# Three-layer FP32 block on one core: weights loaded per 512 KB unit into six slots, x and the first units alternating, the MLP activation kept in PSUM

## What is computed

```python
# layer 0: s = concat(short gated conv, gated DeltaNet) @ w_out_even; x = layer_norm(alpha * x + s)
#          x = x + (p @ w_pl) * sigmoid(x @ w_pl_gate)
# layer 1: the same with an HGRN2 mixer (w_in_odd: 1024 x 8192, w_out_odd: 2048 x 1024)
# layer 2:
h = h + swa_mixer(rms_norm_2(h, attn_norm), ...)     # sliding window attention, 16 heads
a = jax.nn.relu(rms_norm_2(h, mlp_norm) @ w_up)      # 1024 -> 4096
h = h + (a * a) @ w_down                             # 4096 -> 1024
return rms_norm_2(h, final_norm)
```

## Time and profile before

| what | value |
|---|---|
| time, three runs | 1053.04, 1055.29, 1056.65 us, median 1055.29 |
| the profiled execution | 1055.54 us, its span 1053.8 us (1.7 us lie around the span) |
| busy: PE, PEld, DVE, ACT, POOL | 94%, 88%, 42%, 47%, 67% of the span |
| mean granted TensorE clock | 0.987 of full speed |
| DMA | 146.22 MB in 128940 packets, mean 139 GB/s |

### The profile page before, as it was taken

How to read it: one execution, slowest core, us unless ns; L and a number is a source line. 1 busy time by engine, 2 the same in 40 slices (tenths; PEclk the granted TensorE clock), 3 DMA queues, 4 the chain that set the end, 5 groups by cost and what they waited for, 6 DMA issues and landing times.

```text
span 1053.8 us, 18046 instructions
## 1 busy us (share of the span) xinstructions
PE 993.6 (94%) x7200; PEld 929.7 (88%) x7200; DVE 446.5 (42%) x741; ACT 499.6 (47%) x697; POOL 701.1 (67%) x540
## 2 busy tenths in 40 slices
PE   3699999999999999999999999999997989998996
PEld 3699999989999789999999999888886889887884
DVE  1254854358442153444444444435465264442003
ACT  2465432473224465444555545456547444544430
POOL 2776644556445688856666566659672469999992
PEclk9899999999999999999999999999999999999998
DMA  6989954966823555644444434455541145554651
GB/s 180 189 163 127 125 112 82 118 120 105 140 81 120 177 178 161 191 143 122 128 125 131 137 121 132 139 180 173 168 159 41 50 150 162 160 161 160 212 187 40
DMA packets 128940, 146.22 MB, mean 139 GB/s; under 512 B 8974, under 2 KB 93656, under 8 KB 128856
## 3 DMA queue, kind: packets, MB, share of 16 engines
q1 hardware_dynamic: 125432, 140.05, 52.4%
q10 hardware_dynamic: 3424, 5.01, 1.4%
HBM read 144.00 MB, written 1.05 MB: 138 GB/s over the span
## 4 chain that ended last, share of the span: by engine, by line
PE 73%; POOL 10%; issue 6%; DVE 5%; ACT 3%; DMA 3%; SPq 0%; DVEq 0%; ACTq 0%; POOLq 0%
PE dense L484 18%; PE dense L485 18%; PE dense L486 18%; POOL wlo L461 5%; POOL wlo L460 5%; PE bank L839 4%; DMA raw<-in_w_in_even_dram 3%; PE bank L741 2%; PE bank L736 2%; PE bank L740 2%; PE bank L837 1%; PE dense L553 1%; PE bank L885 1%; DVE nsink L1984 1%; ACT whi L1035 1%
## 5 line engine op out<-in xcount | busy, mean ns | idle before, releaser
L460 POOL TENSOR_TENSOR wlo<-raw,whi 128x512 fp32r<-128x512 f32 x264 | 352.2, 1334 | 312.9 <-ACT whi L1035 310.7
L1035 ACT ACTIVATE whi<-raw 128x1024 fp32r<-128x1024 f32 x264 | 275.1, 1057 | 377.6 <-PE dense L486 247.7
L484 PE MATMUL dense<-x_hi,whi 128*128 128x256 f32 x1232 | 364.9, 296 | 26.1 <-POOL wlo L461 18.8
L461 POOL TENSOR_TENSOR wlo<-raw,whi 128x512 fp32r<-128x512 f32 x264 | 357.4, 1354 | 0.0
L485 PE MATMUL dense<-x_lo,whi 128*128 128x256 f32 x1232 | 352.2, 286 | 0.0
L486 PE MATMUL dense<-x_hi,wlo 128*128 128x256 f32 x1232 | 352.2, 286 | 0.0
L484 PEld LDWEIGHTS dense<-x_hi,whi 128*128 128x128 f32 x1232 | 239.9, 195 | 31.5 <-issue 17.4
L485 PEld LDWEIGHTS dense<-x_lo,whi 128*128 128x128 f32 x1232 | 240.1, 195 | 1.8 <-issue 1.7
L486 PEld LDWEIGHTS dense<-x_hi,wlo 128*128 128x128 f32 x1232 | 239.7, 195 | 0.0
L484 PE MATMUL dense<-whi,ya_hi 128*128 128x512 f32 x192 | 77.9, 406 | 2.9 <-POOL wlo L461 2.2
L486 PE MATMUL dense<-whi,ya_lo 128*128 128x512 f32 x192 | 75.0, 391 | 0.0
(11 more groups left out here) (296 smaller groups left out, 1488.9 us busy)
## 6 DMA issues: line engine op xcount, KB each, us to landing
raw<-in_w_in_odd_dram SPq DMA_DIRECT2D x32, 1024.0 KB, 5.8
raw<-in_w_in_even_dram SPq DMA_DIRECT2D x16, 1024.0 KB, 12.3
raw<-in_w_in_even_dram SPq DMA_DIRECT2D x64, 256.0 KB, 6.1
raw<-in_mlp_w_up_dram SPq DMA_DIRECT2D x16, 1024.0 KB, 5.5
raw<-in_mlp_w_down_dram SPq DMA_DIRECT2D x16, 1024.0 KB, 5.0
raw<-in_w_out_even_dram SPq DMA_DIRECT2D x8, 1024.0 KB, 5.0
raw<-in_w_pl_gate_dram SPq DMA_DIRECT2D x8, 1024.0 KB, 5.2
raw<-in_w_out_odd_dram SPq DMA_DIRECT2D x8, 1024.0 KB, 5.1
```

The source lines that it names most:

```text
L460: pool.tensor_tensor(wlo[:, slot, 0:half], unit_slot(u)[:, 0:half], whi[:, slot, 0:half].bitcast(F32), ALU.subtract)
L461: pool.tensor_tensor(wlo[:, slot, half:2 * half], unit_slot(u)[:, half:2 * half], whi[:, slot, half:2 * half].bitcast(F32), ALU.subtract). ...
L484: pe.matmul(out_, lh, rh, start=start, stop=False, skip_group_check=True)
L1035: act.activation(whi[:, u % NSPL, :], unit_slot(u), ACT.Copy).then_inc(hi_done, 1)
```

## The change

Five things.

1. `raw` has six slots of one unit (the same memory), and every load is of one unit: 264 loads of 512 KB in place of 132 of 1 MB (the conv weights stay at 256 KB per DMA, the k and v weights of attention go from 12 DMAs to 24 of half the size). Before the load of unit u SP waits for `lo_done` of unit u-6.
2. At the start SP issues the first half of x, unit 0, the second half of x, units 1 to 5, then the norm rows. PE transposes both halves of x before unit 0, and ACT takes the high parts of the second half after unit 0 (before: after unit 2).
3. The other 928 KB of the constants are issued by ACT in two parts, 512 KB at step 8 and 416 KB at step 40; DVE waits for the first at step 17 and for the second before the HGRN stage. `tail_turn` moves from step 4 to 6, `gates` from 5 to 7.
4. MLP up: DVE computes `max(x, 0) * root` in place in PSUM (2 x 128x512), ACT squares it in place in PSUM and writes the high part, DVE the low part, all by halves, and the pair is freed after the low part. `rl` is gone.
5. For MLP units POOL computes the low part with one instruction of 128x1024.

```diff
...
 COLS = 512
 RAWK = 4
 SPLK = 2
-NRAW = 3
+NRAW = 6
...
-        raw = sb("raw", [P, NRAW, RAWK * COLS])
+        raw = sb("raw", [P, NRAW, SPLK * COLS])
...
-            return raw[:, (u // 2) % NRAW, (u % 2) * SPLK * COLS:(u % 2 + 1) * SPLK * COLS]
-
-        def weights(c):
+            return raw[:, u % NRAW, :]
...
+            def wide(w):
+                return w[part * RAWK * P:(part + 1) * RAWK * P, :].rearrange("(k p) c -> p k c", p=P)
...
         def _(sp):
-            for c in range(2):
+            def load_x(c):
+
+                cols = slice(c * COLS, (c + 1) * COLS)
                 for i in range(NT):
-                    cols = slice(c * COLS, (c + 1) * COLS)
                     sp.dma_start(xtok[:, i, cols], a["x"][0, i * P:(i + 1) * P, cols]).then_inc(x_loaded[c], 16)
-            for n, c in enumerate(LOADS):
-                slot = n % NRAW
-                if n == NRAW:
+
+            load_x(0)
+            for u in range(SPLITS):
+                c, part, slot = LOADS[u // 2], u % 2, u % NRAW
+                if u == 1:
+                    load_x(1)
+                if u == NRAW:
...
-                if n >= NRAW:
-                    sp.wait_ge(lo_done, 2 * (n - NRAW + 1))
+                if u >= NRAW:
+                    sp.wait_ge(lo_done, u - NRAW + 1)
...
-                    w = weights(c)
+                    w = weights(c, part)
                     sp.dma_start(dst.rearrange("p (k c) -> p k c", k=w.shape[1]), w).then_inc(raw_ready[slot], 16)
...
                 slot, half = u % NSPL, SPLK * COLS // 2
-                pool.tensor_tensor(wlo[:, slot, 0:half], unit_slot(u)[:, 0:half], whi[:, slot, 0:half].bitcast(F32), ALU.subtract)
-                pool.tensor_tensor(wlo[:, slot, half:2 * half], unit_slot(u)[:, half:2 * half], whi[:, slot, half:2 * half].bitcast(F32),
+                first = half if u < FIRST_SPLIT[("up", 0, 0)] else 0
+                if first:
+                    pool.tensor_tensor(wlo[:, slot, 0:half], unit_slot(u)[:, 0:half], whi[:, slot, 0:half].bitcast(F32), ALU.subtract)
+                pool.tensor_tensor(wlo[:, slot, first:2 * half], unit_slot(u)[:, first:2 * half], whi[:, slot, first:2 * half].bitcast(F32),
                                    ALU.subtract).then_inc(lo_done, 1)
...
             pe.wait_ge(consts_loaded, 16)
             transposes("x_t", 0, xtok, x_loaded[0], [32, 32], range(1))
+            transposes("x_t", 0, xtok, x_loaded[1], [32, 32], range(1, 2))
...
                     dense_feature("hcbz", (n - FIRST_YA) // 4, n % 4, x_hi, x_lo)
                 else:
                     out_unit("out_even", n - FIRST_OUT)
-                if n == 0:
-                    transposes("x_t", 0, xtok, x_loaded[1], [32, 32], range(1, 2))
                 if n == 1:
                     pe.wait_ge(taps_loaded, 16)
                     pe.transpose(SB[0][:, 0:STACK_A], stA, ident[0:STACK_A, 0:STACK_A]).then_inc(stack_t, 1)
                 if n == 3:
                     tail()
-                if n == 4:
+                if n == 6:
                     tail_turn()
                 if n == 11:
                     pe.wait_ge(stacks_loaded, 128)
...
                         group_start("down", c)
                     for q in range(4):
                         ch = (8 * g + 2 * q) // 4
-                        pe.wait_ge(a_ready, ch + 1)
+                        pe.wait_ge(a_ready, 2 * ch + q % 2 + 1)
                         ah, al = act_tiles(ch)
                         wh, wl = unit_ready()
...
                 while at["unit"] < min(end, SPLITS):
                     u = at["unit"]
-                    act.wait_ge(raw_ready[(u // 2) % NRAW], ready_at[u // 2])
+                    act.wait_ge(raw_ready[u % NRAW], ready_at[u])
                     if u >= NSPL:
                         act.wait_ge(split_used, u - NSPL + 1)
                         act.wait_ge(lo_done, u - NSPL + 1)
...
             act.dma_start(gate_rows[:, 1, :], a["dt_bias"][0:1, :].broadcast_to([P, GH])).then_inc(rows_loaded, 16)
             tables(SILU_TABLES)
             take_hi(xf0, x_hi, 0, range(2))
-            split_until(3)
+            split_until(1)
             take_hi(xf0, x_hi, 0, range(2, 4))
             split_until(AHEAD)
-            act.dma_start(con[:, C_NEG:], consts[:, C_NEG:]).then_inc(consts_loaded, 16)
             act.wait_ge(tail_loaded, 16)
             act.activation(tail_hi[:, :, :], tail_w[:, :, :], ACT.Copy).then_inc(tail_split, 1)
             settle(tail_split)
...
                     if r == 8:
                         conv_gate(p, "v")
                         gain(p)
+                if n == 8:
+                    act.dma_start(con[:, C_NEG:C_PICK], consts[:, C_NEG:C_PICK]).then_inc(consts_loaded, 16)
+                if n == 40:
+                    act.dma_start(con[:, C_PICK:], consts[:, C_PICK:]).then_inc(consts_loaded, 16)
                 if n == 4:
                     act.wait_ge(tail_out, 1)
                     act.activation(hs[0:16, :], SB[1][0:16, 0:T], ACT.Copy).then_inc(tail_rows, 1)
                     settle(tail_rows)
-                if n == 5:
+                if n == 7:
                     gates()
                 for j in range(KT):
                     r = n - FIRST_YA - 4 * j
...
             take_hi(xf, x_hi, 4)
             rstd(1, RMS_EPS)
-            for c in range(9):
-                if c < 8:
-                    split_until(FIRST_SPLIT[("up", c, 0)] + 4 + AHEAD)
-                    group_ready("up", c)
-                    bank = pair_of("up", c)
-                    if c - 1 > 0:
-                        act.wait_ge(a_ready, c - 1)
-                    for b in range(2):
-                        act.activation(rl[:, c % 2, 2 * b * T:2 * (b + 1) * T], bank[b][:, :], ACT.Relu).then_inc(relu_done, 1)
-                        settle(relu_done)
-                    act.sem_inc(pair_free[PAIR[("up", c)]], 1)
-                if c >= 1:
-                    if c > 0:
-                        act.wait_ge(squared, c)
-                    act.activation(act_tiles(c - 1)[0], rl[:, (c - 1) % 2, :].rearrange("p (k t) -> p k t", k=4), ACT.Copy).then_inc(a_hi_done, 1)
+            for c in range(8):
+                split_until(FIRST_SPLIT[("up", c, 0)] + 4 + AHEAD)
+                bank = pair_of("up", c)
+                for b in range(2):
+                    act.wait_ge(relu_done, 2 * c + b + 1)
+                    link(act.activation(bank[b][:, :], bank[b][:, :], ACT.Square))
+                    act.activation(act_tiles(c)[0][:, 2 * b:2 * b + 2, :], bank[b][:, :].rearrange("p (k t) -> p k t", k=2), ACT.Copy).then_inc(a_hi_done, 1)
                     settle(a_hi_done)
             split_until(SPLITS)
             for i in range(NT):
...
                 settle(ya_ready)
                 free("hcbz", j)
-            vec.wait_ge(consts_loaded, 32)
             for n in range(GD_STEPS):
-                if n == 5:
+                if n == GDN_FIRST[0]:
+                    vec.wait_ge(consts_loaded, 32)
+                if n == 7:
                     gates()
                 if n == 12:
                     vec.wait_ge(stack_t, 2)
...
                 if k == 1:
                     free("qf", p)
+            vec.wait_ge(consts_loaded, 48)
             for g in range(HG_STEPS):
                 for p in range(HH // 2):
                     r = g - 8 * p
...
             residual("o_att", 1.0, turn=lambda c: take("mlp_t", 0, xf, x_hi, x_lo, 4, MLPN, parts=range(2 * c, 2 * c + 2)))
             row_stats(True)
             take_root_row(2)
-            link(vec.tensor_tensor(root[:, :], root[:, :], root[:, :], ALU.mult))
-            for c in range(9):
-                if c < 8:
-                    vec.wait_ge(relu_done, 2 * c + 2)
-                    link(vec.tensor_tensor(rl[:, c % 2, :], rl[:, c % 2, :], rl[:, c % 2, :], ALU.mult))
-                    four_tiles = rl[:, c % 2, :].rearrange("p (k t) -> p k t", k=4)
-                    vec.tensor_tensor(four_tiles, four_tiles, root[:, :].unsqueeze(1).broadcast_to([P, 4, T]), ALU.mult).then_inc(squared, 1)
-                    settle(squared)
-                if c >= 1:
-                    if c > 0:
-                        vec.wait_ge(a_hi_done, c)
-                    hi, lo = act_tiles(c - 1)
-                    vec.tensor_tensor(lo, rl[:, (c - 1) % 2, :].rearrange("p (k t) -> p k t", k=4), hi.bitcast(F32),
+            for c in range(8):
+                group_ready("up", c)
+                bank = pair_of("up", c)
+                for b in range(2):
+                    tiles = bank[b][:, :].rearrange("p (k t) -> p k t", k=2)
+                    vec.scalar_tensor_tensor(tiles, tiles, 0.0, root[:, :].unsqueeze(1).broadcast_to([P, 2, T]), ALU.max, ALU.mult).then_inc(relu_done, 1)
+                    settle(relu_done)
+                hi, lo = act_tiles(c)
+                for b in range(2):
+                    vec.wait_ge(a_hi_done, 2 * c + b + 1)
```

(3 more changed lines are left out.)

29 lines of the change are left out of this document (14 added, 15 removed).

## The result

| | before | changed |
|---|---|---|
| median of 4 runs beside each other | 1055.97 us (1053.04 to 1057.11) | 1030.39 us (1029.21 to 1031.01) |
| ratio to before, 95% interval | 1 | 0.9761 [0.9738, 0.9783] |
| span of the profiled execution, mean granted clock | 1053.8 us, 0.987 | 1029.2 us, 0.993 |
| PE busy | 993.6 us (94%) | 987.0 us (96%) |
| POOL busy, instructions | 701.1 us, 540 | 669.4 us, 476 |

The account below looks back on a forecast made before the run. PE, busy 94%, was held by 21.0 us of waits on POOL's low parts: the DMA stream at the start, slow POOL halves in the MLP. 12 + 10 = 22 us off 1055.5 gives 1033.5 us, range 1027 to 1043.5.

Parts of the forecast that it names:

- Whole low parts. 0: MLP on POOL: one 128x1024 instruction takes 2.4 to 2.6 us, PE needs 2.7 or more, so no gain.
- Loads of one unit. I count 0: Weight stream: five units of lead, 13.5 us, cover 4.3 us landing plus 3.6 for split and low part; 0 gained.
- unit 9 lands at 40.1 in place of 45.5: Start: 0.95 MB of constants out of the queue at 177 GB/s brings unit 9 earlier by 5.4 us.
- 1.7 us were taken off for a clock that did not fall: Start: 1.7 us deducted from a 13.5 us gain for half-speed PE work after idling, leaving 12 us.
- 5.4 us for the constants: Start: moving 0.95 MB of constants later saves 5.4 us of stream time ahead of unit 9.
- The order of x: Start: PE begins unit 0 at about 16 to 17.6 in place of 19.77, never returning to wait for x (3.19 us).
- A: Stream falls behind again between units 12 and 18, or brings unit 9 late; 1040.5 us, chance 0.13.
- B: MLP gains nothing: PE waits for the pair of PSUM banks instead of for POOL; 1043.5 us, chance 0.08.
- D: Loads of 512 KB do not overlap as those of 1 MB did, 4.3 us a unit; slower, 1142 us, chance 0.04.
- the 1072 us beside it: Kernel time if DMA fixed parts did not overlap: skill formula's 3.2 us per MLP unit in place of 2.75.
- C: Both upper bounds, 16.2 us at the start and 11.5 in the MLP, are reached; 1028 us, chance 0.07.
- E: Neither part gains: start waits move to `k_sums_of`, the lock on POOL stays; 1055 us, chance 0.02.

Follow-up runs that it names:

- t1: Changed kernel plus three unused DVE additions of 128x1024, SBUF to SBUF, after each MLP up group; ratio 0.9812, MLP 176.5 us.
- t2: Changed kernel plus six unused DVE additions of 128x512 with one operand in PSUM after each MLP up group; ratio 0.9772, MLP 170.8 us.
- u2: Changed kernel with POOL's low parts of the MLP units in two halves again, activation kept in PSUM; ratio 0.9759, MLP 170.7 us.
- u7: Changed kernel with both MLP parts undone: activation through the SBUF tile and low parts in halves; ratio 0.9862, MLP 182.0 us.
- u1: Changed kernel with the MLP activation alone back through an SBUF tile, whole low parts kept; ratio 0.9826, MLP 176.1 us.
- u6: Changed kernel with weights loaded in 1 MB pairs again from unit 2 on; ratio 0.9852, start 150.2 us, MLP 170.8 us.
- u8: Changed kernel with early constants, old order of x and first units, and old gates step together; loads of one unit kept; ratio 0.9858, start 149.1 us.
- u3: Changed kernel with the 928 KB of constants in one early transfer behind the fifth split, as before; ratio 0.9804, start 146.9 us.
- u4: Changed kernel with x and the first units in the order of before on SP, ACT and PE; ratio 0.9815, start 146.1 us.
- u5: Changed kernel with the turning of the tail and the gates back at their old steps, 4 and 5; ratio 0.9834, start 147.2 us.

## Why the prediction was right, and where it was not

**The total held, and the MLP held in its mechanism.** 1033.5 was forecast and 1030.39 measured, inside the range; 22 us were forecast off the profiled execution and 24.5 came (1055.54 to 1031.01). For the MLP, 10 us forecast and 10.9 measured; no low part over 2.43 us, DVE's operations at 0.69 to 0.70 us, POOL with slack and PE without a wait, as the marks of the prediction ask. t1 and t2 show the cause apart from the change. *The Trainium skill*, page "SBUF — State Buffer", section "SBUF: two separate sides", says that a DVE operation with two SBUF inputs and a GpSimd operation that reads SBUF exclude each other for a whole instruction, whichever starts first. The traces agree on both sides of it: POOL's mean low part goes from 2.41 to 3.05 us beside such operations, DVE's from 2.20 to 3.31 when POOL's instruction doubles in length, and with one operand in PSUM both are untouched. "**Whole low parts. 0**" is right for the change as it is (u2), and would be 5.9 us wrong without the activation in PSUM (u7 against u1).

**The step that failed is "Loads of one unit. I count 0".** They are worth 8.4 us by the marks and 9.6 by the ratios (u6 against the changed kernel), more than any other single edit of the start; u8 against before gives 7.5 by the marks and 4 by the times. I priced them in the steady state only, by the time to land against five units of lead, and there 0 is right. At the start there is no lead: what counts is when a unit lands and when its slot can be asked for again. The step on the constants is wrong with it: "unit 9 lands at 40.1 in place of 45.5" was credited to 0.95 MB fewer bytes. With the constants late and loads in pairs (u6) the split stands at 42.56; with the constants early and single loads (u3) at 40.61; both together bring 37.23. So the constants were given 5.4 us of landing where u3 shows 3.4, the loads nothing where u6 shows 5.3, and 1.7 us were taken off for a clock that did not fall (1.00 from 46.5 to 60). Unit 6 began at 40.44, outside the 43 to 45 of the prediction and at its upper bound of 40.7, PE's own work: 16.5 us gained there against 12. Of these 1.7 us are given back by the last key sum, 1.1 of them in a new wait of PE for DVE, which leaves 14.8. That the start came within 3 us is luck in part: one term too large stood in for one put at nothing.

**"5.4 us for the constants"** met 5.1 (u3). The path is the prediction's, the squares behind the split of unit 9, and not the low part that u3's expectation named; but the split moves by 3.4 us only, and the rest comes with PE's idle time and the lower clock after it. **The order of x** I had as 2 to 4 us at the first unit and nothing of its own at unit 6; it is 4.3 (u4). **The gates' step** was not priced at all, and is 5.4 (u5). I had read the 4.75 us wait before `tail_turn` as a result of the late stream alone.

**The single prices are no shares.** Each of the four edits of the start costs 4.3 to 8.4 us when it alone is missing (the marks of unchanged starts scatter by 2.5), 23.2 us in sum, and the whole gain is 14.8. PE passes unit 5 when two chains have both arrived: its own progress (x, units 0 to 5), and ACT's (landing of unit 9, its split, squares, copy). u3 and u5 delay the second, u4 the first, u6 both; whichever is later sets the time, and what delays the other is then free, as u8 shows.

**Of the rivals**, A did not come: no wait on low parts between 60 and 90 us, though the stream ran at 140 GB/s there, where by the prediction's sum no cover is left. B did not either: no wait of PE for the pair of banks is in the list. D falls with u6's MLP column. So does the 1072 us beside it, worked out from the formula of *The Trainium skill*, page "DMA: Bandwidth & Descriptors"; that formula stands in the section "Anatomy of one DMA — SWDGE (gpsimd) path", for DMAs that GpSimd issues, while SP issues the loads here, and the MLP's 512 KB loads landed 4.0 (up) and 4.7 us (down) after issue, at 192 GB/s over MLP up, where one after the other at 3.2 us each they would bring 164. C, both upper bounds, 1028, is nearer than the forecast in both terms (14.8 of 16.2, 10.9 of 11.5, a bound for which the prediction gives no working); the 1.6 us given back in attention stand in none of the cases. E fails at each of its points.

**What stays open**: the time between the two `root` rows, 99.8 to 106.3 us, over kernels with one and the same program there. The profiles differ in PE's waits on `pt` (2.8 us in the changed kernel, 7.2 before and in u2 and t1, 5.1 in u8), which do not follow the length of the stage, and in the granted clock (0.92 to 0.98), which explains a part at most: u1 and u2 both have 0.97, at 105.3 and 103.3 us. None of the twelve runs was aimed at it. This is where the runs of one kernel differ by some microseconds and where the changed kernel's profile gave 1.6 us back. Open too is which of a pair's two drawbacks costs the most at the start, the later request or the later landing of its first unit.

## What to carry to other kernels

Price a smaller load twice: in the steady state, where it may be worth nothing, and at a start, where the first use waits for the last byte of a transfer and the next request for the whole slot. Where several edits aim at one wait, undo each alone and then all at once: the single losses can sum to more than the whole (23.2 against 14.8 us here), and the difference tells which chains run side by side. Where GpSimd paces a stage, look for DVE operations that read SBUF twice, and put one operand in PSUM before anything else is tuned.

## What the runs showed of the hardware that was not expected

- DVE's 128x1024 operation on SBUF took 2.20 us beside POOL's halves of 1.29 us and 3.31 us beside whole parts of 2.41 us; POOL lost 2.6 us a group in both. The longer instruction of POOL shifts the waiting to DVE and costs POOL nothing more. A 128x512 operation of DVE took 0.71 us with POOL idle and 2.77 us beside low parts of 2.8 us (changed kernel, 842.73 and 833.25).
- POOL's 128x1024 low part takes 2.41 us, two halves 2 x 1.29 = 2.59 us: 0.18 us a unit. Over the 32 units of MLP up that makes an estimated 5.8 us, and 5.9 were measured where POOL paces the stage (u7 against u1).
- Four small loads (64 KB in rows of 64 bytes, 48 KB, twice 4 KB) issued at the start hold the first 8 us to 108 GB/s; without them it is 191. Issued later, behind more loads in flight, they take ACT 5.9 us instead of 3.4 to issue.
- After a wait of 4.1 us (u3) and one of 5.1 us (u5) PE ran for some 5 to 7 us at a granted clock of 0.50 (1.2 GHz), a mean of 0.67 from 40 to 50 us; the changed kernel, with waits of at most 1.1 us there, stays at 1.00 (2.4 GHz). Such a wait costs more than its own length: in u3 it is 4.1 us, with 2.6 us of other waits gone, and 5.1 us are lost.
